# Other fixed merge orders for the pieces of a pair turn in a two-layer RWKV-7 / Conformer / gMLP backbone on one core

## What is computed

```python
def step(S, inp):
    w_t, k_t, v_t, kk_t, kka_t = inp[:5]
    sa = jnp.einsum('bhvk,bhk->bhv', S, kk_t)
    S = (S * w_t[:, :, None, :] - sa[..., None] * kka_t[:, :, None, :]
         + v_t[..., None] * k_t[:, :, None, :])
    y = jnp.einsum('bhvk,bhk->bhv', S, inp[5]) if want_y else None
    return S, y
...
for d, rev in enumerate((False, True)):
    dec_c, kd_c, kka_c = dirs_c[d]
    s_ctx, yc = wkv_scan(s0, dec_c, kd_c, v_c, kk_c, kka_c, r_c, rev)
    dec_x, kd_x, kka_x = dirs_x[d]
    _, yx = wkv_scan(s_ctx, dec_x, kd_x, v_x, kk_x, kka_x, r_x, rev)
```

## Time and profile before

| | value |
|---|---|
| median of 3 runs | 4474.54 us |
| profiled execution, its own time | 4475.39 us |
| its span, first to last instruction | 4473.6 us |
| TensorE busy | 4219.4 us, 94% |
| VectorE busy | 1365.3 us, 31% |
| ScalarE busy | 1074.1 us, 24% |
| pair turns 2 to 7 of layer 0 | six stretches from 256.2 to 945.7 us |
| turn 8 of layer 0 | 945.7 to 1043.6 us |
| pair turns 2 to 7 of layer 1 | six stretches from 2714.6 to 3378.6 us |
| turn 8 of layer 1 | 3378.6 to 3474.0 us |

### The profile page before, as it was taken

One profiled execution on the slowest core, in us unless ns is written; L12 is line 12 of the kernel. 1 busy time (PEld: TensorE's weight loads), 2 busy tenths in 40 slices (PEclk: granted clock), 3 DMA queues, 4 the chain that ended last, 5 costly groups with the idle time before them and its releaser, 6 DMA issues. The chain is left out here.

```text
span 4473.6 us, 108758 instructions
## 1 busy us (share of the span) xinstructions
PE 4219.4 (94%) x51156; PEld 2514.7 (56%) x51156; DVE 1365.3 (31%) x2121; ACT 1074.1 (24%) x1778; POOL 58.1 (1%) x52
## 2 busy tenths in 40 slices
PE   7999999988999999999999989999997899999998
PEld 3566666665555555555555556666666344444443
DVE  1555555554730000100000255555554220010000
ACT  2444444442020000100000244444443120010000
POOL 0000000000000000000000000000000000000000
PEclk8999999988999999999999989999998999999999
DMA  5000000003431111111111200000000532222222
GB/s 187 23 8 23 23 22 23 27 20 125 135 124 52 52 49 52 42 52 52 52 52 52 84 23 8 22 21 22 21 31 13 199 111 76 78 68 75 75 80 75
DMA packets 67388, 260.42 MB, mean 58 GB/s; under 512 B 7680, under 2 KB 9984, under 8 KB 66048
## 3 DMA queue, kind: packets, MB, share of 16 engines
q1 hardware_dynamic: 62208, 219.18, 15.4%
q10 hardware_dynamic: 3456, 29.04, 1.6%
q0 software_dynamic: 1280, 5.24, 0.3%
HBM read 239.80 MB, written 13.63 MB: 57 GB/s over the span
## 5 line engine op out<-in xcount | busy, mean ns | idle before, releaser
L584 PE MATMUL psum<-arena,ring 128*128 128x512 f32 (+1 forms) x4992 | 1805.0, 523 | 29.4 <-ACT arena L1326 22.6
L584 PEld LDWEIGHTS psum<-arena,ring 128*128 128x128 f32 x4992 | 950.5, 191 | 890.0 <-issue 816.0
L879 PE MATMUL psum<-arena 32*32 32x32 f32 (+4 forms) x40512 | 835.0, 212 | 147.0 <-issue 112.0
L879 PEld LDWEIGHTS psum<-arena 32*32 32x32 f32 (+3 forms) x40512 | 753.4, 122 | 336.8 <-issue 269.4
L766 PE MATMUL psum<-arena,ring 128*128 128x512 f32 (+1 forms) x1408 | 554.3, 523 | 2.5 <-ACT arena L1419 1.6
L1254 PE MATMUL psum<-arena,ring 128*128 128x512 f32 (+1 forms) x1440 | 520.2, 521 | 0.0
L1254 PEld LDWEIGHTS psum<-arena,ring 128*128 128x128 f32 x1440 | 273.6, 190 | 242.0 <-issue 229.6
L766 PEld LDWEIGHTS psum<-arena,ring 128*128 128x128 f32 x1408 | 254.2, 194 | 201.6 <-issue 178.3
L2161 DVE TENSOR_TENSOR arena<-psum,arena 128x768 f32<-128x768 f32 (+1 forms) x44 | 36.3, 825 | 718.8 <-PE psum L584 718.8
L2102 DVE TENSOR_TENSOR arena<-psum,arena 128x768 f32<-128x768 f32 (+1 forms) x48 | 39.6, 825 | 617.9 <-PE psum L584 617.9
L1698 ACT ACTIVATE arena<-psum 128x768 f32<-128x768 f32 (+1 forms) x44 | 31.0, 704 | 698.8 <-PE psum L584 698.8
(11 more groups left out here) (131 smaller groups left out, 2464.2 us busy)
## 6 DMA issues: line engine op xcount, KB each, us to landing
ring<-w_stream_in SPq DMA_DIRECT2D x408, 512.0 KB, 3.7
x_spill<-arena ACTq DMA_DIRECT2D x2, 3072.0 KB, 8.7
arena<-ya_spill ACTq DMA_DIRECT2D x2, 3072.0 KB, 10.0
arena<-x_spill ACTq DMA_DIRECT2D x2, 3072.0 KB, 18.5
ring<-w_stream_in ACTq DMA_DIRECT2D x8, 512.0 KB, 6.3
arena<-x_in ACTq DMA_DIRECT2D x1, 3072.0 KB, 14.3
arena<-ups_in SPq DMA_DIRECT2D x16, 192.0 KB, 2.4
ya_spill<-arena POOLq DMA_DIRECT2D x8, 384.0 KB, 6.8
```

Source lines behind the costliest of these rows:

```text
L584: mm = eng.matmul(psum[0:lhs[k].shape[-1], tile, a - off:b - off], lhsT=lhs[k], rhs=rhs[k][:, a:b], start=(k == 0), stop=(k == len(lhs) - ...
L879: return pe.matmul(out, lhsT=lhs, rhs=rhs, start=start, stop=stop, skip_group_check=True)
```

## The change

All eighteen strings are replaced by others with the same letters in the same numbers, so the order inside a generator stays, and only the merge differs. Nothing else is changed. For the two TensorE strings of turns 2 to 7 (layer 0 and layer 1):

```diff
 WEAVE.update((("PE", 0, t), (
-    "xxdddssxxsddssxxsdddxxdddsxsdddddsdddssdddssxdxsdddsddddddsdddssdddsxddsdddsdddsdddsxxdddsxxdddssddd"
-    "sssssddssssssssdddssssddssssssssssssssssssssdssssssss")) for t in range(2, KT))
+    "dxxssxddsdxxssdxdsxdddxdsdxsdddddsdddsddsddsxxsdddsddsddsddsddsdddddsxdsdddsdddsdddsdxxddsxddxsssdds"
+    "sddssddssssssssdddsssdssssssdsssssssssssssssdssssssss")) for t in range(2, KT))
...
 WEAVE.update((("PE", 1, t), (
-    "xxssxsxsxsxsddddddxsdsdddsddddddssxddddsdsddddddsdddddssdsdsdssxdsdddsddddddsxxddddsxxxsxsxsssssssdd"
-    "dssssssddsssssssssssssssssssssssssssssss")) for t in range(2, KT))
+    "xdsssxxssxsxdddxddsxdsdddsdddddsddxdddsdsddsdddsddddsddsdsdsdsdxsdddssxxxsxddsxdddxdsssxdsssdsddssss"
+    "sssddssssdsddsssssssssssssssssssssssssss")) for t in range(2, KT))
```

More of the change, by code:

```diff
@@ L164 @@
 WEAVE.update((("PE", 0, t), (
[L165 removed]
+    "xxddddddxsxsdxxsddssxxsxddxdddxdxddxsxdddsdssdddddsddddsddsddddsdsdssdddsdsddsdddsxddsddddsddxsddddd"
     "sssssssssssssssssssssssssssssssssssssssssssssss")) for t in (1,))
 WEAVE.update((("PE", 0, t), (
[L168 to L169 removed]
@@ L170 @@
[L170 to L174, removed]
@@ L175 @@
-WEAVE.update((("V", 0, t), "ttttssstssstsssstssspsptsssssppssssspsppsspsspssspsspppssssssppsppssssppstsssstssststspspsppspstspp") for t in range(2, KT))
-WEAVE.update((("V", 0, t), "tsstssssttstssstsssttssssstststsssstssssssssssssssssssssssssssssssssssss") for t in (KT,))
+    "dxxssxddsdxxssdxdsxdddxdsdxsdddddsdddsddsddsxxsdddsddsddsddsddsdddddsxdsdddsdddsdddsdxxddsxddxsssdds"
+    "sddssddssssssssdddsssdssssssdsssssssssssssssdssssssss")) for t in range(2, KT))
+WEAVE.update((("PE", 0, t), "xxsxsxssdxssxxxdsxdsxddssddsxssdssssssssssxxsxxssxsssssssssssssssssssssssssssssssssssssssssssss") for t in (KT,))
@@ new lines @@
+WEAVE.update((("A", 0, t), "xxxxxxssspxxxxsssssxpxpxpppppppppxppppppppxpsssxspsssspssspsssssssssss") for t in (1,))
+WEAVE.update((("A", 0, t), "xxxssxsxxsssxssxppxpppppxpppxpppppxpsssxxpppsxssxppssppsspsppspssssspsssss") for t in range(2, KT))
+WEAVE.update((("A", 0, t), "xxxxsxsssxssxssxxxppppxsxssxsxssxxssssssssssssssss") for t in (KT,))
+WEAVE.update((("V", 0, t), "tssstttsstsptsssssssppsspspssssspspspsssppssspspspstspsspspppssspsppsppsssspppsssssssssssssss") for t in (1,))
+WEAVE.update((("V", 0, t), "ttsttsstssstssstssspstssspssppssssssssppsspspsspsppsssspspssspsppssspsppstsssstssststspspsppspstspp") for t in range(2, KT))
@@ L177 @@
+WEAVE.update((("V", 0, t), "tsstssssttstssstsssttsssssttststssssssssssssssssssssssssssssssssssssssss") for t in (KT,))
 WEAVE.update((("PE", 1, t), (
-    "xxdddddxssxxsdddssxsdxxddddsxxsdddsdddssdxsddddddsdddddsssdxsdsdsdssddddddsddddddsxxdddsxdssxsssssss"
+    "dxdddxddxsxsssdxsxdsdxxddddsxxsdddsdddsdsxsddddddsdddsddssdxsdsdsddssddddddddsddddsdxxdsxdsxssssssss"
     "sssssssssssssssssssssssssssssssssssss")) for t in (1,))
 WEAVE.update((("PE", 1, t), (
-    "xxssxsxsxsxsddddddxsdsdddsddddddssxddddsdsddddddsdddddssdsdsdssxdsdddsddddddsxxddddsxxxsxsxsssssssdd"
@@ L187 @@
-WEAVE.update((("V", 1, t), "tsssttsssttsssssssppsssppssssppsspssppsstsssspspsssppppsspppsssppspppspssssssssssssssssss") for t in (1,))
-WEAVE.update((("V", 1, t), "tsssstssttsssssstsstssppssssppssppsspspspsssspsspssssppppsssppspppspsspsppststssstssstsssssss") for t in range(2, KT))
-WEAVE.update((("V", 1, t), "ttstssstsstssssssstsssssttsstsssssssssssssssssssssssssssssssssssssss") for t in (KT,))
+    "xdsssxxssxsxdddxddsxdsdddsdddddsddxdddsdsddsdddsddddsddsdsdsdsdxsdddssxxxsxddsxdddxdsssxdsssdsddssss"
@@ new lines @@
+    "sssddssssdsddsssssssssssssssssssssssssss")) for t in range(2, KT))
+WEAVE.update((("PE", 1, t), "xxssdsxxssxxsdxsxxsssxxsdsdsssxsssssssxxsssxsxssssssssssssssssssssssssssssssssssssssssssss") for t in (KT,))
+WEAVE.update((("A", 1, t), "xxxxxxssssssssxpxpxppppppppxpxpppppppppxppsxxsssxsspxssssssssssssssss") for t in (1,))
+WEAVE.update((("A", 1, t), "xxxsxsssssxsspxppxppppppppxpppxppxppxxsppsssxppxpsxssxspsspssssssssssssp") for t in range(2, KT))
+WEAVE.update((("A", 1, t), "xxxssxssxxsssspxxxppxxxssssxxssxsxsssssssssssssss") for t in (KT,))
@@ L192, in weave @@
+WEAVE.update((("V", 1, t), "tssstsststtsssssssspsssppsspssppsspssppstsspspssssppsppsspppsssppsppspspsssssssssssssssss") for t in (1,))
+WEAVE.update((("V", 1, t), "tsssstssttssssssststpsspsspspspsssssppspsspsspspsssssppsppssspppppstsspstspsssssssssppstsssst") for t in range(2, KT))
+WEAVE.update((("V", 1, t), "ttsssttssstsssssstssssssssststssssstssssssssssssssssssssssssssssssss") for t in (KT,))
 def weave(order, **streams):
```

## The result

| | before | after |
|---|---|---|
| median | 4475.18 us, 4 runs (4472.16 to 4481.23) | 4423.50 us, 4 runs (4418.83 to 4432.48) |
| profiled execution, its own time | 4475.39 us | 4424.15 us |
| its span | 4473.6 us | 4422.3 us |
| turns 2 to 7 of layer 0 | 689.5 us | 669.0 us |
| turns 2 to 7 of layer 1 | 664.0 us | 635.1 us |

The ratio is 0.9885 with a 95% interval of 0.9866 to 0.9904: 51.7 us faster, where 35 were forecast. Of the 51.3 us by which the spans differ, 20.5 lie in turns 2 to 7 of layer 0, 28.9 in those of layer 1, 1.1 in the two turns 8, 0.8 elsewhere.

What follows compares the result with a forecast made beforehand. TensorE's own list was taken to bound the pairs phase. Gaps -10 -12, waits -8, clock -7 -8, switches +3 +8, turns 1 and 8 -1 sum to -35: 4475.4 to 4440 us, 8-in-10 range 4418 to 4466.

Steps and rivals of the forecast that it cites:

- the clock: Turns 2 to 7: fewer falls to 1.2 GHz after large gaps, -7 us in layer 0 and -8 in layer 1.
- likeliest case: The prediction's own sum of terms for the whole kernel, 4425 to 4452 us, chance 0.47.
- Gaps at the borders of blocks: TensorE's issue gaps at 256-instruction borders shrink under dense work: -10 us in layer 0, -12 in layer 1.
- Place B: Layer 1, fourth level's last two inversion pieces adjoin: up to 2.2 us of new gap; over 2 us would show it wrong.
- Waits on other engines, layer 1: Place C, state sums and fourth hop: k-tiles ahead of them cover waits for VectorE and ScalarE, -8 us.
- Switches: Added borders between dense and small work, 17 a turn in layer 0 and 20 in layer 1: +3 and +8 us.
- fourth rival: At the 17 and 20 new borders a turn, switches cost more than charged, 49 us: 4501 us, chance 0.08.
- Turns 8: Turn 8 has hardly any dense work to move, so its gaps stay; with turn 1, -1 us.
- The first: Rival: gaps shrink but the clock still falls, so 15 us of gain are missing: 4455 us, chance 0.22.
- The second: Rival: all turns lose their falls of the clock and most gaps, -63 us: 4412 us, chance 0.12.
- The third: Rival: gaps are a fixed cost of a block, independent of cover, and stay: 4478 us, no change, chance 0.11.

Runs made afterwards that it cites:

- three kernels with shifted borders: Kernel before, orders unchanged, with satisfied waits added on TensorE's queue ahead of layer 0's and/or layer 1's turns: 4467.73, 4482.61 and 4536.92 us.
- place A alone: Kernel before with only letters 34 to 56 of TensorE's order changed, turns 2 to 7 of layer 0: 4444.44 us, ratio 0.9930.
- place C alone: Kernel before with layer 1's changed ScalarE and VectorE orders, and TensorE's changed only from letter 71 (blocks and hops): 4467.98 us, ratio 0.9994.
- last three mixtures: Changed kernel's layer 1 with 65 altered first letters; layer 0 with letters 34 to 56 changed, 19 to 56, or all: 4418.34, 4416.20, 4417.16 us.

## Why the prediction came out as it did

The mechanism was as written; one term, the clock, was less than half its true size (-15 us for some -35). That is more than the whole of the missing 17 us, and dearer switches took a little of it back. The 4423.5 us lie in the range that was given, 1.5 us below the band of the likeliest case.

**Gaps at the borders of blocks.** Layer 0: -13 us measured (28.7 to 15.7) for -10. Layer 1: -8 (35.2 to 27.5) for -12. That they belong to borders of 256 instructions is shown by the three kernels with shifted borders, where they moved by 102, 128, 51, 204 and 102 instructions with the borders. The count of transfers fits as well: 2 x 51156 matmuls and weight loads and 1342 semaphore instructions make 405 blocks of 256. That cover shrinks them is shown by place A alone.

**Place B.** The prediction had a gap of over 2 us there as what would make it wrong. It nearly came, with 1.99 us in turn 5 and 1.94 in turn 2, beside one of 2.1 to 2.2 us ahead of it in the same turns. Those turns take 109.9 and 108.1 us with falls of the clock, the third and sixth 102.9 and 102.6 without. Most of the fall belongs to the gap ahead: behind place B the clock was low for 3.4 us in turn 5 and not at all in turn 2. These gaps are the larger part of why layer 1's shrank less than forecast.

**Waits on other engines, layer 1.** The earlier trace rows and a few shorter ones made 15.5 us; 3.5 are left, of which 2.3 are new, for the copy at L1382. So -12 for -8. The run of place C alone says that this is not net: there 14 us of the old waits and 3 us of issue went, 5.9 us of busy time and a new wait of 6.3 us took 12 back, and 5 in all are left. In layer 0 small waits of 1.9 us are new.

**The clock.** This is the term that was mis-sized. The prediction took 1.8 us a turn in layer 0 from two groups, the 64x512 product and the transposes. But the low stretch holds 5.86 us of busy time at 0.50, which is 2.9 at full clock: the loss is up to 2.9 us a turn, and the rows said so. Then it took 7 of 11 us, where all six falls went. At clock 1.00 turn 3 takes 107.16 us of busy time with place A alone, with two switches more than before, for 109.65 before. With 0.3 us for the switches that is 2.8 us, 17 us in six turns, for -7.

In layer 1 the prediction priced the two long turns against one of 107.8 us, as if that one had no fall of its own. It had, and so had all six turns:

```profile
2873.50:2880.20 6.70, 4.88 (x201) 3.31 (x203) 2.28 (x5) 0.00 (x0) 0.00 (x0) 0.50 0.01 2
```

So 12.7 us was not all that the clock cost there. What it did cost is an estimate. Before, the turns with the least low clock (0.98) had 99.2 and 99.5 us of busy time and about 1.6 of it lost, so some 97.7 at full clock, 586 for six, and 612.0 - 586 = 26 us of loss. After, the undisturbed turns had 98.8 to 99.1, so 601.5 - 594 = 8. That is -18 for -8. A second estimate agrees with both: each instruction in a low stretch against the same one in other kernels with the same order, where the clock was 1.00, gives a loss of 17 us before and none after in layer 0, 25 before and 7 after in layer 1.

**Switches.** A switch costs 0.17 us where it is added alone. But the change's 17 and 20 more in a turn cost far less than 17 and 20 of those. In layer 0 busy time at full clock grows from some 106.8 to 108.0 us a turn, +7 us for the +3 charged; in layer 1 by 1.2 a turn, +7 for +8. That many switches take the place of costs already paid fits this, and it is what kept the fourth rival from coming: its place, the 37 borders, cost some 14 us in all and not 49.

**The sum.** Layer 0: -13 - 17 + 7 + 2 = -21 (20.5 measured). Layer 1: -8 - 12 - 18 + 7, and 1 us more in pauses below 0.15 us, = -30 (28.9 measured). Turns 8: -1, as forecast. That is -52 (51.3 measured), for -35. Gaps and waits together came out nearly as forecast (-31 for -30), but by luck within them: waits of layer 1 and gaps of layer 0 gave more than forecast, gaps of layer 1 less. The clock came out at -35 for -15, switches and small pauses 4 us dearer.

**The rivals.** The first (the clock stays) is refuted in layer 0 and was true of three turns of layer 1. The second (everything evens out, 4412) was the nearest of them in time, 12 us off, and not in kind, since the gaps stayed at 43 us and three turns of layer 1 kept falls of the clock. The third is refuted by place A alone, where the borders stood at the same counts and the gaps shrank. (Its stretch without a gap from 406.44 to 427.35 has 508 matmul records, so four blocks, where the prediction gave time for five.) It was also the way of the Trainium skill's section on instruction fetch mechanics ("Runtime: NRT & Kernel Launch"), by which a refill is mostly hidden; here a block's refill stands in the open where its 256 instructions run shorter than some 4 us, and 204 instructions of shift made 32 us of difference in six turns. The fourth did not come, as said above.

What stays open: why a like gap brings the fall in one run and not in the next. Nor was the changed order run with its borders shifted, so how much of its 51 us hangs on where they lie isn't shown. In the last three mixtures the same orders had two to four turns of layer 1 with a fall. In the second one the clock fell in turn 3 with no gap over 0.7 us near. Busy time around that fall:

```profile
2844.00:2851.20 7.20, 5.33 (x199) 3.00 (x200) 4.63 (x8) 4.12 (x7) 0.00 (x0) 1.00 0.03 5
2851.30:2858.10 6.80, 6.80 (x205) 4.44 (x204) 2.23 (x4) 2.60 (x4) 0.00 (x0) 0.75 0.02 5
```

TensorE was busy 5.33 of the 7.20 us ahead, its idle time in several short waits. So a single large gap is not needed for a fall, and in turn 7 of place A alone one of 2.32 us was not enough.

## What to carry to other kernels

Where an engine executes many tiny instructions, look at the spacing of its "issue" gaps, counted in instructions: if it is constant, look whether the engine waits for its own instruction blocks. Here it did, and long instructions put between runs of short ones won both most of the gap and the clock that fell with it. Price a low-clock stretch by all its busy time at half clock, from one row of busy time, not by a few groups in it, and take that as an upper bound: a piece of 48 small products took 1.50 us for 1.02 in the low stretch of turn 5 of layer 1 after the change, less than twice. Compare only with a turn that has no low stretch itself. And such an order is tuned to where the borders lie: anything that adds or takes away instructions ahead of it moves them, here with -11 to +32 us in six turns for the same order, so measure again after any such edit, and don't credit the edit with it.

## What the runs showed of the hardware

- The same orders took 678.6, 689.5 and 721.1 us for six turns when the borders of the blocks were 102, 0 and 204 instructions earlier.
- Two waits on a satisfied semaphore in a row took one place in the block of instructions, and in a row of 172 such places each took 0.11 us on TensorE.
- In the three runs with shifted borders the 19 to 29 issue gaps of over 0.3 us in turns 2 to 7 of a layer stood within one instruction of one and the same place in the block of 256.
- Each of the 51 such gaps of the kernel before ended 1.1 to 1.5 us after a transfer of the instruction queue had ended.
- A switch between a k-tile and small products cost 0.17 us (six of them 1.03 us) in a stretch of TensorE without a wait.
